# Expert rows of layer 1 fetched by indirect transfers and turned, in place of a product with the pick matrix

## The reference, cut to what matters

```python
h = _modulate(_rmsnorm(x, norm_ffn_g[layer]), sh_f, sc_f)
# top 1 of 4 groups, top 2 of its 4 experts: gates (T, 16), two nonzero entries in a row
out = jnp.zeros_like(t)
for e in range(N_EXPERTS):
    he = jax.nn.silu(t @ w1[e]) * (t @ w3[e])
    out = out + gates[:, e:e + 1] * (he @ w2[e])
```

## Time and profile before

| what | us |
|---|---|
| median of 3 runs | 955.0 (953.03 to 955.36) |
| profiled execution, its own time | 954.5 |
| its span, first to last instruction | 952.7 |
| TensorE matmul busy | 848.1 (89%) |
| VectorE, ScalarE, GpSimd busy | 303.4, 191.3, 150.9 |
| mean granted TensorE clock | 0.956 |

### The profile page before, as it was taken

How to read it: one execution, slowest core, us unless ns; L and a number is a source line. 1 busy time by engine, 2 the same in 40 slices (tenths; PEclk the granted TensorE clock), 3 DMA queues, 4 the chain that set the end, 5 groups by cost and what they waited for, 6 DMA issues and landing times.

```text
span 952.7 us, 12757 instructions
## 1 busy us (share of the span) xinstructions
PE 848.1 (89%) x5229; PEld 463.9 (49%) x5230; DVE 303.4 (32%) x708; ACT 191.3 (20%) x310; POOL 150.9 (16%) x244
## 2 busy tenths in 40 slices
PE   3799998799999998999687999699999899999993
PEld 0367644565465553554544543434444554654641
DVE  1337432541130410311799610620000311301314
ACT  1403330421221311312400100310101212213111
POOL 3201019185443445300000000000000000000000
PEclk9799999789999999999799999789999899999997
DMA  9999999439999999996997682207775299999961
GB/s 306 346 382 276 343 384 360 164 130 400 392 399 402 393 398 400 392 392 245 395 337 263 214 310 87 98 2 259 275 261 186 106 398 392 396 397 391 393 248 68
DMA packets 126288, 285.32 MB, mean 299 GB/s; under 512 B 7092, under 2 KB 8388, under 8 KB 125992
## 3 DMA queue, kind: packets, MB, share of 16 engines
q1 hardware_dynamic: 119392, 276.83, 78.9%
q0 software_dynamic: 1984, 5.21, 1.9%
q10 hardware_dynamic: 4872, 2.72, 1.0%
HBM read 279.50 MB, written 5.24 MB: 299 GB/s over the span
## 4 chain that ended last, share of the span: by engine, by line
PE 75%; DVE 10%; DMA 7%; ACT 2%; issue 2%; SPq 2%; ACTq 1%; DVEq 0%
PE PS L1578 19%; PE PS L1597 13%; PE PS L1605 8%; PE PS L1621 7%; PE PS L1581 6%; PE PS L1866 5%; PE PS L1324 4%; PE PS L1418 3%; DMA yg<-in_s_c_im 3%; DMA ring<-in_moe_w 2%; DMA work<-in_ada_w 2%; PE PS L1349 2%; DVE work L1289 2%; PE PS L1401 2%; SPq L339 1%
## 5 line engine op out<-in xcount | busy, mean ns | idle before, releaser
L1597 PE MATMUL PS<-ring,work 128*64 128x512 f32 (+1 forms) x512 | 130.5, 597 | 6.2 <-ACT work L772 6.2
L1578 PE MATMUL PS<-ring,hT 128*64 128x256 f32 x896 | 108.4, 383 | 2.5 <-DMA ring<-in_moe_w 2.5
L1578 PE MATMUL PS<-ring,yg 128*64 128x256 f32 x896 | 107.4, 381 | 0.0
L1578 PEld LDWEIGHTS PS<-ring,hT 128*64 128x64 f32 x896 | 66.5, 137 | 40.0 <-issue 8.5
L1597 PEld LDWEIGHTS PS<-ring,work 128*64 128x64 f32 (+1 forms) x512 | 43.1, 143 | 85.4 <-issue 85.4
L1211 DVE TENSOR_TENSOR work<-work,PS 128x512 f32<-128x512 f32 x32 | 22.0, 687 | 194.9 <-PE PS L1578 146.9
L1605 PE MATMUL PS<-work,xhat 128*128 128x256 f32 (+1 forms) x256 | 76.9, 453 | 7.0 <-issue 6.9
L1578 PEld LDWEIGHTS PS<-ring,yg 128*64 128x64 f32 x896 | 68.1, 138 | 29.7 <-issue 0.9
L1215 DVE COPY yg<-PS 128x512 f32<-128x512 f32 x32 | 22.1, 692 | 180.5 <-PE PS L1597 180.5
L1621 PE MATMUL PS<-yg,grow 64*128 64x512 f32 (+1 forms) x256 | 70.1, 612 | 7.1 <-DVE yg L1215 7.1
L1605 PEld LDWEIGHTS PS<-work,xhat 128*128 128x128 f32 x256 | 49.2, 207 | 38.8 <-issue 22.1
(11 more groups left out here) (345 smaller groups left out, 978.3 us busy)
## 6 DMA issues: line engine op xcount, KB each, us to landing
ring<-in_moe_w SPq DMA_DIRECT2D x96, 2048.0 KB, 16.7
ring<-in_ada_w SPq DMA_DIRECT2D x20, 2048.0 KB, 15.0
work<-in_ada_w SPq DMA_DIRECT2D x4, 2048.0 KB, 13.8
ring<-in_s_glu_w SPq DMA_DIRECT2D x4, 2048.0 KB, 16.6
ring<-in_ab_w_in SPq DMA_DIRECT2D x3, 2048.0 KB, 21.9
ring<-in_ab_w_out SPq DMA_DIRECT2D x2, 2048.0 KB, 13.6
rot_tables<-work POOLq DMA_DIRECT2D x16, 256.0 KB, 5.7
ring<-rot_tables SPq DMA_DIRECT2D x2, 2048.0 KB, 11.1
```

What stands on the lines that cost most here:

```text
L1578: last = mm(dst[64 * u:64 * u + 64, 0:256], hg[k][:, e * P:e * P + 64], w[:, k, 256 * u:256 * u + 256], start=k == 0, stop=k == KD - 1)
L1597: last = mm(dst, heT[:, at:at + (64 if narrow else P)], w[:, c4, h * HALF:(h + 1) * HALF], start=c4 == 0, stop=c4 == KF - 1)
```

## The change

Layer 1 alone. GpSimd zeroes `picked` (four experts x 1024 columns, in space that S5 has left), stores the normalized rows to device memory once (`xhat_rows`, 1 MB), and then fetches, for each group, four times up to 128 rows by an indirect transfer, one for each expert: the row number of slot `s` stands in `row_no[s, e]`. A slot without a token has a number out of bounds and is left alone. The numbers come from a product: `pick` (stationary) by a column of token numbers minus 4096, to which VectorE adds 4096 and casts. For the first group TensorE makes them ahead of the loop; for group `i + 1` between up(3) and down(2) of group `i`, and VectorE converts them between gated(3) and y_out(2). The gather's products give way to transposes of the fetched rows (`turn_rows`), into the same banks and with the same evacuations. On GpSimd, `over_row(1)` comes behind the first group's four fetches. Waits that are added: the gather waits for its group's four transfers (`picked_in`); GpSimd waits for the row numbers and, from the second group on, for the gather that read `picked` before.

```diff
@@ -137,6 +138,8 @@
         rti = sb("rti", [P, 2 + NG], I32)
+        row_no = sb("row_no", [P, EPG], I32)[:, :]
+        token = sb("token", [P, NB])[:, :]
         slotv = sb("slotv", [P, P])[:, :]
@@ -201,6 +204,8 @@
         MTMP = 0
+        picked = w3(T0, EPG, D)
+        xhat_d = nc.dram_tensor("xhat_rows", [T, D], F32).ap()
         hg_lo = hT[:, :, :].rearrange("p k t -> p (k t)").rearrange("p (k n) -> p k n", n=HALF)
@@ -435,7 +440,9 @@
                    allow_small_or_imprecise_dtypes=True).then_inc(S("consts_ready"), 1)
-            pool.wait_ge(S("consts_ready"), 2)
+            g.iota(token, pattern=[[P, NB]], base=-NO_ROW, channel_multiplier=1,
+                   allow_small_or_imprecise_dtypes=True).then_inc(S("consts_ready"), 1)
+            pool.wait_ge(S("consts_ready"), 3)
             pool.dma_start(rti[:, 0:NB], a["positions"][0].rearrange("(b p) -> p b", p=P),
@@ -566,7 +573,27 @@
             pool.sem_inc(S("h0_ready"), 1)
+
+            pool.wait_ge(S("s5_ps"), KD)
+            g.memset(picked, 0.0).then_inc(S("picked_zero"), 1)
+            pool.wait_ge(S("xhat_ready"), 2 * 3 + 2)
+            pool.dma_start(xhat_d.rearrange("(b p) n -> p b n", p=P), xhat[:, :, :]).then_inc(S("xhat_stored"), 16)
+            pool.wait_ge(S("picked_zero"), 1)
+            pool.wait_ge(S("xhat_stored"), 16)
+
+            def fetch_rows(group):
+
+                pool.wait_ge(S("row_no_ready"), group + 1)
+                if group:
+                    pool.wait_ge(S("gathered"), KD * (NG + group))
+                for e in range(EPG):
+                    g.indirect_dma_start(picked[:, e, :], None, xhat_d, bass.IndirectOffsetOnAxis(ap=row_no[:, e:e + 1], axis=0),
+                                         bounds_check=T - 1, oob_is_err=False).then_inc(S("picked_in"), 16)
+
+            fetch_rows(0)
             over_row(1)
+            for group in range(1, NG):
+                fetch_rows(group)
 
@@ -1191,9 +1218,16 @@
 
+                def row_numbers(done):
+
+                    dve.wait_ge(S("row_no_ps"), done)
+                    v.tensor_scalar(row_no, bank[0][:, 0:EPG], float(NO_ROW), None, ALU.add).then_inc(S("row_no_ready"), 1)
+
                 slots(krow[:, 0, :])
                 link(v.tensor_copy(kcur, krow[:, 0, :]))
+                if L == 1:
+                    row_numbers(1)
 
@@ -1231,6 +1265,8 @@
                     gated(3)
+                    if L == 1:
+                        row_numbers(2 + i)
                     y_out(2)
@@ -1606,6 +1642,20 @@
 
+            def number_rows():
+
+                for e in range(EPG):
+                    for b in range(NB):
+                        last = mm(bank[0][:, e:e + 1], pick[:, b, e, :], token[:, b:b + 1], start=b == 0, stop=b == NB - 1)
+                last.then_inc(S("row_no_ps"), 1)
+
+            def turn_rows(k, narrow):
+
+                for e in range(EPG):
+                    n_s = 64 if narrow and e else P
+                    last = tr(bank[k % 2][:, e * P:e * P + n_s], picked[0:n_s, e, k * P:(k + 1) * P], n_s)
+                return last
+
             def turn_weights():
@@ -1660,6 +1710,10 @@
                 pe.wait_ge(S("narrow_known"), L + 1)
+                if L == 1:
+                    pe.wait_ge(S("pick_ready"), 5 * L + 1)
+                    pe.wait_ge(S("picked_zero"), 1)
+                    number_rows()
 
@@ -1669,10 +1723,18 @@
                         pe.wait_ge(S("he_ready"), 1 + e0)
+                        if L == 1:
+                            pe.wait_ge(S("picked_in"), 16 * EPG + i * (16 * EPG))
                         for k in range(KD):
                                 pe.wait_ge(S(("hg_act", "hg_dve")[k % 2]), 4 * gi + k // 2)
-                            gather_block(k, narrow).then_inc(S("gathered"), 1)
+                            (gather_block if L == 0 else turn_rows)(k, narrow).then_inc(S("gathered"), 1)
+
+                    def next_rows():
+
+                        pe.wait_ge(S("pick_ready"), 5 * L + i + 2)
+                        pe.wait_ge(S("sil_ready"), 1 + e0 + EPG)
+                        number_rows()
 
@@ -1731,6 +1793,8 @@
                         up(3, narrow)
+                        if L == 1:
+                            next_rows()
                         down(2, narrow)
@@ -1751,6 +1815,8 @@
                     pe.wait_ge(S("pick_ready"), 5 * L + 5)
+                    if L == 1:
+                        pe.wait_ge(S("row_no_ready"), NG + 1)
                     for k in range(KD):
```

More of the change, by code:

```diff
@@ L48 @@
 TWO_PI = (6.28125, 0.0019340515136718750, 1.2556659817695618e-06)
+NO_ROW = 4096
 SLOTS = 6
@@ L1331, in _ @@
             tr(bank[2][:, 0:KD], crow, KD).then_inc(S("c_ps"), 1)
-            pe.wait_ge(S("consts_ready"), 2)
+            pe.wait_ge(S("consts_ready"), 3)
             pe.wait_ge(S("pool_order"), 4)
```

## The result

The changed kernel takes 961.6 us, median of 4 runs (960.46 to 962.65), the one before 954.8 in 4 runs beside it: a ratio of 1.008, with an interval of 1.0063 to 1.0098. It is slower by 6.8 us. The changed kernel's profiled execution took 960.46 us, its span 958.7, and the mean granted clock fell from 0.956 to 0.941.

A forecast was written before the change was run, and what follows sets the result against it. TensorE was taken to set the end, with DMA in reserve. 5.3 + 7.0 - 1.3 - 4.8 = +6.2 us on the profiled 954.5 gave 960.7, and 0.5 more for the median 961 us; range 956 to 971.

The forecast's parts named there:

- first group: Layer 1's wide group: numbers, fetch and low-clock turning start the up product effectively at 643.6 against 638.3, +5.3 us.
- second group: First narrow group, at the low clock before and after: gather 9.9 us before, 8.6 after, -1.3 us.
- third and fourth group: Last two narrow groups, at full clock: gathers of 8.04 us each fall to 5.6, -4.8 us together.
- numbers in the loop: Token-number products between up(3) and down(2), four times 16 passes of 0.11 us, paid in full on TensorE: +7.0 us.
- The fetch: Ahead of the first group: four indirect transfers, 10.0 us from conversion to landing, bounds 6.6 and 15.
- rival D: A quick first fetch, 6.7 us or less, leaves the kernel within 0.3% of before; chance 0.15.
- Half of such a stretch is lost, 1.9 us: First group's up product starts at the low clock and loses half of a 3.9 us stretch, 1.9 us.
- Rival B: The clock falls in the third and fourth groups' turned gathers and returns only in the up product: 967 us; chance 0.25.
- sign of being wrong: Forecast wrong if an indirect issue costs several microseconds, the clock falls in every turned stretch, or number passes run beside others.
- The reserve of DMA: Weight loads stay ahead of TensorE by some 7.5 us at the smallest; a limit if narrow groups shorten by over 3.5.
- rival C: Later fetches land late, two taking over 15 us beside the streaming weights: 974 us; chance 0.13.
- the rows' traffic: Fetched rows, 512 of 4 KB or 2 MB, were to take under 3 us of the weights' reserve.

The follow-up runs named there:

- e9: The changed kernel, but the narrow groups' transposes take all 128 rows of each expert, in place of 64 for three of four: 956.63 us, 1.0038 to the kernel before.
- e6: The changed kernel with token numbers by one-pass bf16 products and gathers through four PSUM banks: 950.5 us, 0.9968 to the kernel before.
- e10: e6 with whole transposes of 128 rows in the narrow groups: 948.34 us, 0.9952 to the kernel before.
- e3: The changed kernel, but with token numbers made by one-pass bf16 products in place of fp32: 952.93 us, 0.9996 to the kernel before.
- e8: The changed kernel with bf16 token numbers and four PSUM banks, only the first group fetched and turned, narrow groups gathering by product: 947.18 us, 0.9941 to the kernel before.
- e5: The kernel before, without any fetch, its gathers rotating through four PSUM banks in place of two in both layers: 950.74 us, 0.9974 to the kernel before.

## Why the prediction was right, and where it was not

The forecast was 961 us and the kernel took 961.6, and it is slower, as forecast. That it came so near is in part luck. The sum was +6.2; the medians say +6.8, or 8.3 to 8.7 against the larger batches, and the traces +9.4 from the seeds' end on. The profiled execution reached that point 3.4 us earlier than the one before, ahead of the change. And two terms were wrong in opposite directions: the first group lost 2.1 us less than forecast, the third and fourth gave back 4.7 less.

| step | predicted | measured in the traces |
|---|---|---|
| first group | +5.3 | +3.2 |
| second group | -1.3 | -0.9 |
| third and fourth group | -4.8 | -0.1 |
| numbers in the loop | +7.0 | +7.3 |
| sum | +6.2 | +9.5, against +9.4 from end to end |

The measured terms are seeds' end or gather's start to the up product, plus what the up product takes over its 13.73 or 7.06 us: 20.99 + 0.27 against 18.05; 7.29 + 1.69 against 9.88; 6.77 + 1.46 and 6.03 + 1.75 against 8.04 each; the numbers 1.68 + 3 x 1.88.

**The fetch** went as written, down to its bounds. GpSimd and VectorE in the timeline after:

```profile
620.47 0.16 DVE L1224 TENSOR_SCALAR row_no<-PS 128x4 int32<-128x4 f32 x1 [4.47 <-PE PS L1649]
621.61 1.10 POOL L590 DMA_INDIRECT work<-xhat_rows,row_no  x1 [20.46 <-DVE row_no L1224]
...
625.63 0.99 POOL L590 DMA_INDIRECT work<-xhat_rows,row_no  x1 [0.30 <-issue]
```

An issue is 1.0 us with 0.3 behind it, GpSimd starts 1.0 us after the conversion, and the rows are in 5.16 us after the last issue began: 10.2 us from conversion to landing, predicted 10.0. That too is partly luck: the parts are 1.0 + 3 x 1.34 + 5.16, where I had 3 x 1.1 + 6.7. The Trainium skill's page "DMA: Bandwidth & Descriptors", section "Anatomy of one DMA — SWDGE (gpsimd) path", gave an estimate of 3.2 us for such a transfer; this trace does not agree, with 5.16, and rival D, which needed a total of 6.7 or less, is out. The overflow row came behind the issues, as said, and held nobody up. The 16 slow passes of numbers took 3.52 us (3.8).

**What was mis-sized in the first group** is the low clock behind the fetch. "Half of such a stretch is lost, 1.9 us" took the up product for the place where the clock comes back. It came back inside the turning:

```profile
632.00:634.00 2.00, 1.98 (x10) 1.41 (x9) 0.81 (x1) 0.79 (x2) 0.00 (x0) 0.50 0.00 0
634.00:635.00 1.00, 0.84 (x6) 0.60 (x5) 0.31 (x1) 0.75 (x1) 0.00 (x0) 0.83 0.00 0
635.00:636.00 1.00, 0.91 (x8) 0.64 (x7) 0.50 (x1) 0.50 (x1) 0.00 (x0) 1.00 0.00 0
```

The up product then lost 0.27 us. The sum of the low clock's turn was also slightly off: 0.65 + 0.15 + 0.83 is 1.63 us and not 1.68, and for the wide block 1.75 and not 1.8; the turned gathers took 7.02 us here and 7.29 in the second group. The page "TensorE: Matmul & The Clock Gate" of the Trainium skill, section "Part 4: PE-mode transpose", says that full clock does not engage for transposes. These rows and e9 do not agree for whole fp32 transposes of 128 rows; those with 64 rows behave as the page says.

**The step that failed** is "Third and fourth, full clock: before 8.04 each, after 5.6". Two things in it were wrong. A transpose with 64 rows costs no less than a whole one: a turn is 1.53 us at full clock, not 1.40, so the price was just above the upper bound of 1.50. And the clock did not stay full. Rival B named this and had 0.25; from the stretches after:

```profile
814.00:815.00 1.00, 1.00 (x8) 0.66 (x7) 0.38 (x1) 0.49 (x1) 0.00 (x0) 1.00 1.05 387
815.00:816.00 1.00, 0.75 (x5) 0.44 (x4) 0.81 (x1) 0.29 (x1) 0.00 (x0) 0.62 1.04 385
816.00:817.00 1.00, 1.00 (x7) 0.66 (x6) 0.00 (x0) 0.64 (x1) 0.00 (x0) 0.50 1.06 395
...
821.00:822.00 1.00, 1.00 (x8) 0.53 (x6) 1.00 (x5) 0.00 (x0) 0.00 (x0) 0.50 0.99 393
822.00:823.00 1.00, 1.00 (x12) 0.60 (x10) 0.76 (x5) 0.00 (x0) 0.00 (x0) 0.96 1.02 389
...
883.00:884.00 1.00, 0.82 (x7) 0.49 (x9) 0.66 (x1) 0.98 (x2) 0.00 (x0) 0.76 1.06 408
```

In the third group the clock is at 1.00 in the first blocks, falls near 815.2, and is back only near 822, inside the up product. In the fourth the whole gather ran at 1.00, 6.03 us as in e9; the clock fell near 883.5, as the up product began, and was back near 887. So rival B is true of the third and fourth group, though not in all of its price. Of the 4.7 us by which the forecast missed -4.8, the clock cost 4.0 (0.74 in the third gather's turns, 1.46 and 1.75 in the up products), where B said 6; the dearer turns cost the rest. By its own sign of being wrong, a clock that falls in every turned stretch, the forecast was nearly so: it fell, or stayed low, in or right behind all three narrow gathers, and rose only in the wide one. The time stayed below B's 967 because the clock cost less than 6 us, the first group was 2.1 us cheaper, and the stretch ahead of the experts came out 3.4 shorter in the profiled execution. Rival B's reason, sparse transposes, is not the right one: e6 has them dense and loses the clock, e9 has them sparse and keeps it. What tells the two apart is the shape, 64 rows against 128, and e10 beside e6 says the same with four banks. Whether the half-filled rows or the 64 columns that move do it stays open; a block with only one of the two halved was not run.

**The numbers** cost what the nearest rows said, in full: 7.3 us on TensorE's line in four places (7.0), 0.105 to 0.118 a pass. e3 shows it from the other side.

**The reserve of DMA** held: rival C did not happen (the last issue began at 866.94, the gather that reads those rows at 877.4, and no narrow gather waits for DMA), and TensorE waits for no weights in the narrow groups. But the reserve was smaller than I said. "DMA would become a second limit if a narrow group got shorter by over 3.5 us": in e6 the period was 61.9 us (748.69 to 810.57), 1.2 less than before, and TensorE already waited 1.7 us; in e10 it was 59.4, 3.7 less, and the waits came to 7.0. One term behind it is the rows' traffic, "under 3 us". The row of the fetches' queue on the page after (packets, MB, share of 16 engines' span):

```profile
q0 software_dynamic: 4560, 9.29, 3.1%
```

and on e8's, which lacks the three later fetches:

```profile
q0 software_dynamic: 2832, 7.42, 2.5%
```

3.1% of 958.7 less 2.5% of 945.5 us is an estimated 6 us of all 16 engines (a unit of the last digit is 1 us) for the three fetches that run beside the weights. That is twice what I had said and most of the 7.5 in reserve. e8, with only the first fetch, runs its narrow periods in 62.2 us and waits for no weights there. That the traffic is what used up the reserve is argued from these numbers; a fetch of fewer bytes was not run.

**The better version** is e8: the rows fetched and turned in the wide group alone, where the product with the pick matrix takes 15.9 us at its best and the turning 6.1 behind 10 us of fetch, the numbers in bf16, four banks for every gather, and the product kept in the narrow groups. At 947.18 us it is 0.6% under the kernel before; 2.5 of those 6.1 us e5 has without any fetch. e10 cannot be told from it, as the intervals overlap.

## What to carry to other kernels

A small product is priced by its passes, not by its columns: an index made with one moving column still loads a full stationary operand twice in fp32, so where the operands are exact in bf16, use it. Replace a matrix product by a transfer and transposes only where the product is long and the fetch's 10 us can be hidden or is outweighed, and read the granted clock in the product that follows, since a shorter stretch can hand its gain to its successor. Do not cut a transpose down to the rows in use without measuring: here whole ones were cheaper, by 5.0 us in e9. Before shortening every group of a streaming loop, work out the reserve of the queue that feeds it; it caps the sum of all such gains.

## What the runs showed of the hardware

- A pass with a 128x128 stationary operand and one moving column takes 0.105 to 0.118 us in fp32 and at most 0.044 in bf16 at full clock (1.68 and 1.88 over 16, 0.35 over 8); at the low clock fp32 takes 0.22 (3.52 over 16).
- Gathers with three transposes of 64 rows in a block let the granted clock fall from 1.00 to 0.50, in the gather or as the next product began (after, e3, e6); with whole ones it stayed at 1.00 (e9, e10), and rose from 0.50 in the wide group.
- Back to back at full clock, 28 transposes of whole rows take 3.22 us (e10), and 28 of which three in four have 64 rows 4.15 (e6).
- The rows out of bounds are counted as read: the page's HBM reads rose from 279.50 to 287.89 MB, 8.4 MB, which is 16 x 128 rows of 4 KB, and to 281.60 in e8, 2.1 MB for 4 x 128 rows; only 512 rows have a token. The queue's own row grows by 4.1 MB (5.21 before, 9.29 after), 1.05 of it the store, so whether all those bytes were moved stays open.
- Ahead of the second group TensorE issues nothing for 4.8 us, before the change (4.75) as after it (4.80); with eight more products in the narrow code it was 11.2. The cause was not tried by itself.
